# Query norm of a hybrid decoder step, moved from a stage of its own into the mixing projection

## What is computed

```python
def rms_norm(x, g):
    y = x * rsqrt(mean(x * x, axis=-1) + 1e-6)
    return y * g
...
h = x + merged @ w_mix_out                      # mixing projection, 1024 x 1024
q = rms_norm(h, norm_mem_q_g) @ w_q             # queries, 1024 x 1024
s = (q . k) * 256 ** -0.5 ; p = softmax(s)      # 4 heads of 256, 256 memory rows
h = h + (p . v) @ w_o
h = h + hier_moe(rms_norm(h, norm_ffn_g), ...)  # 32 experts, all weights are read
```

## Time and profile before

| | |
|---|---|
| time, median of 3 runs | 1238.07 us (1235.44 to 1240.53) |
| profiled execution, its own time | 1244.22 us |
| its span | 1242.5 us |
| PE busy | 1159.0 us, 93% |
| DVE busy | 497.1 us, 40% |
| ACT busy | 317.6 us, 26% |
| HBM read | 286.76 MB |

### The profile page before, as it was taken

How to read it: one execution, slowest core, us unless ns; L and a number is a source line. 1 busy time by engine, 2 the same in 40 slices (tenths; PEclk the granted TensorE clock), 3 DMA queues, 4 the chain that set the end, 5 groups by cost and what they waited for, 6 DMA issues and landing times.

```text
span 1242.5 us, 16696 instructions
## 1 busy us (share of the span) xinstructions
PE 1159.0 (93%) x6784; PEld 755.6 (61%) x6784; DVE 497.1 (40%) x876; ACT 317.6 (26%) x602; POOL 54.2 (4%) x83
## 2 busy tenths in 40 slices
PE   4999999999989899987889999999999999999995
PEld 3787568987759899987877874333333333333331
DVE  4989857018754544554445432111121121112103
ACT  3042123233225434543343331111101111011002
POOL 1504000010000000000000000000000000000000
PEclk9999999999859899989899989999999999999998
DMA  9381431033314276352245638999999999999961
GB/s 273 82 220 69 169 135 70 1 117 119 102 51 152 73 280 232 137 182 90 90 177 208 255 154 343 422 421 422 421 421 420 421 421 421 421 421 421 420 285 42
DMA packets 90695, 297.74 MB, mean 240 GB/s; under 512 B 20973, under 2 KB 30921, under 8 KB 65916
## 3 DMA queue, kind: packets, MB, share of 16 engines
q1 hardware_dynamic: 87844, 288.25, 60.5%
q0 software_dynamic: 2256, 7.80, 1.9%
q10 hardware_dynamic: 520, 0.62, 0.1%
HBM read 286.76 MB, written 9.90 MB: 239 GB/s over the span
## 4 chain that ended last, share of the span: by engine, by line
issue 70%; PE 22%; DVE 5%; ACT 1%; DMA 0%; ACTq 0%; POOL 0%; DVEq 0%; POOLq 0%
PE bank L1240 7%; PE bank L1249 2%; PE bank L1225 2%; PE bank L1397 2%; PE bank L1526 2%; PE bank L1520 1%; PE bank L1402 1%; PE bank L1374 1%; PE bank L1443 1%; PE bank L1312 1%; PE bank L1510 1%; DMA work<-in_ssd_d_dram 0%; ACTq L735 0%; DVE work L1949 0%; PE bank L1345 0%
## 5 line engine op out<-in xcount | busy, mean ns | idle before, releaser
L1780 PE MATMUL bank<-ring,work 128*64 128x512 f32 x752 | 200.4, 598 | 0.1
L1547 PE MATMUL bank<-ops,usplit 128*128 128x320 f32 x416 | 132.8, 319 | 11.9 <-DVE usplit L2248 4.9
L1240 PE MATMUL bank<-work,ring 128*128 128x320 f32 (+1 forms) x512 | 136.6, 425 | 0.5 <-DVE work L1949 0.5
L1548 PE MATMUL bank<-ops,usplit 128*128 128x320 f32 x416 | 131.9, 317 | 0.0
L1549 PE MATMUL bank<-ops,usplit 128*128 128x320 f32 x416 | 131.7, 317 | 0.0
L1240 PEld LDWEIGHTS bank<-work,ring 128*128 128x128 f32 x512 | 97.2, 192 | 34.7 <-issue 2.6
L1780 PEld LDWEIGHTS bank<-ring,work 128*64 128x64 f32 x752 | 58.2, 136 | 95.1 <-issue 93.4
L2248 DVE TENSOR_TENSOR usplit<-ring,usplit 128x2048 fp32r<-128x2048 f32 x34 | 77.9, 2291 | 85.1 <-ACT usplit L946 84.7
L1795 PE MATMUL bank<-ring,work 128*64 128x512 f32 x400 | 106.0, 597 | 0.7 <-ACT work L1157 0.7
L1780 PE MATMUL bank<-work 128*64 128x512 f32 x272 | 90.3, 597 | 0.0
L1547 PEld LDWEIGHTS bank<-ops,usplit 128*128 128x128 f32 x416 | 81.3, 195 | 12.9 <-issue 12.7
(11 more groups left out here) (457 smaller groups left out, 1567.1 us busy)
## 6 DMA issues: line engine op xcount, KB each, us to landing
ring<-in_w_exp_down_dram SPq DMA_DIRECT2D x50, 1024.0 KB, 13.9
ring<-in_w_exp_gate_dram SPq DMA_DIRECT2D x49, 1024.0 KB, 13.8
ring<-in_w_exp_up_dram SPq DMA_DIRECT2D x45, 1024.0 KB, 15.2
ring<-in_w_in_dram SPq DMA_DIRECT2D x11, 2048.0 KB, 8.2
work<-in_w_exp_up_dram SPq DMA_DIRECT2D x19, 1024.0 KB, 14.5
work<-in_w_exp_gate_dram SPq DMA_DIRECT2D x15, 1024.0 KB, 15.9
work<-in_w_exp_down_dram SPq DMA_DIRECT2D x14, 1024.0 KB, 12.3
ring<-in_w_glu_dram SPq DMA_DIRECT2D x4, 2048.0 KB, 9.1
```

Source lines behind the costliest of these rows:

```text
L1240: ins = nc.tensor.matmul(b[:, 0:N], wv[:, k, P * (m % 4):P * (m % 4 + 1)], src[:, k, 0:N], start=(k == 0), stop=(k == KT - 1))
L1547: nc.tensor.matmul(b[:, 0:T], wh, hi_[:, k], start=(k == 0), stop=False)
L1548: nc.tensor.matmul(b[:, 0:T], wh, lo_[:, k], start=False, stop=False)
L1780: ins = nc.tensor.matmul(psum[part][ES * x:ES * (x + 1), :], xs[i % 2][:, kk, x], wt[x][:, k], start=(kk == 0), stop=(kk == KT - 1))
```

## The change

The rows are no longer scaled before they are turned. As soon as a mixing unit is added to `h`, ScalarE squares its part of the rows, TensorE turns the two blocks of 128 features that the unit made (`rows_in`, jobs `fq`), ScalarE writes block times gain as the high part and VectorE the low part, both out of the bank. The queries are made of these unscaled rows. The root is taken meanwhile, put on the diagonal of three 128x128 tiles (`diag`), and spread over all partitions by a product with ones (job `rsb`); ScalarE copies that with the factor 1/16, and VectorE multiplies each finished query by it while emptying its bank. Queries 0 and 1 first do blocks 0 to 5, then, when blocks 6 and 7 have been turned, the rest. The first sample's keys are turned after the first scores, and the third sample's load waits until the last query was emptied.

```diff
@@ plan()
-    j += [f"mx{u}{c}" for u in range(4) for c in range(NC)]
-    j += [f"hq{c}{h}" for c in range(NC) for h in range(2)]
-    j += [f"q{m}" for m in range(4)] + [f"kt0{i}" for i in range(4)] + [f"q{m}" for m in range(4, KT)]
-    j.append("sc0")
+    for u in range(4):
+        j += [f"mx{u}{c}" for c in range(NC - (u == 3))]
+        if u:
+            j += [f"fq{2 * u - 2}", f"fq{2 * u - 1}"]
+    j += [f"mx3{NC - 1}", "q0", "fq6", "fq7", "q1", "rsb"] + [f"q{m}" for m in range(2, KT)]
+    j += ["sc0"] + [f"kt0{i}" for i in range(4)]
@@ SyncE
-                if BLOCKS[n][0] == "q0":
-                    sp.wait_ge(s["glu_used"], KT)
-                    load_memory(2)
+            done(sp, f"q{KT - 1}")
+            load_memory(2)
@@ ScalarE
-            for i in range(4):
+            def rows_hi(k):
+                got(act, f"fq{k}")
+                act.activation(q_hi[:, k], bank(f"fq{k}")[:, 0:T], ACT.Copy, scale=vec[:, V_Q + k:V_Q + k + 1]).then_inc(
+                    s["q_hi"], 1)
+
+            for i in range(3):
                 split_unit(unit_of("mx0") + i + 1)
-
+                for c in range(NC):
+                    unit_squares("mx", 0, i, c)
+                if i:
+                    rows_hi(2 * i - 2)
+                    rows_hi(2 * i - 1)
+            split_unit(unit_of("q0"))
             sqrt_table()
-            done(act, f"mx3{NC - 1}")
-            squares(act, 5)
+            unit_squares("mx", 0, 3, 0)
+            unit_squares("mx", 0, 3, 1)
+            rows_hi(4)
+            rows_hi(5)
+            unit_squares("mx", 0, 3, 2)
             root(2)
-            for c in range(NC):
-                for hf in range(2):
-                    done(act, f"hq{c}{hf}")
-                    v = (slice(None), slice(4 * hf, 4 * hf + 4), slice(P * c, P * c + ROWS[c]))
-                    act.activation(q_hi[v], hn2T[v], ACT.Copy).then_inc(s["q_hi"], 1)
+            rows_hi(6)
+            rows_hi(7)
+            split_unit(unit_of("q0", 1))
+            got(act, "rsb")
+            emptied(act.activation(rsb, bank("rsb")[:, 0:T], ACT.Copy, scale=1.0 / 16), "rsb")
...
-            for m in range(KT):
-                if m % 2 == 0:
-                    split_unit(unit_of("q0") + m // 2 + 1)
-                if m == 4:
-                    keys(0)
-                got(act, f"q{m}")
-                emptied(act.activation(qT[:, m], bank(f"q{m}")[:, 0:T], ACT.Copy, scale=1.0 / 16), f"q{m}")
+            for i in range(1, 4):
+                split_unit(unit_of("q0") + i + 1)
             split_unit(unit_of("o0", 1))
+            keys(0)
@@ TensorE
+            def rows_in(k):
+
+                b = take(f"fq{k}")
+                for c in range(NC):
+                    done(pe, f"mx{k // 2}{c}")
+                    ins = tr(b[:, P * c:P * c + ROWS[c]], h[0:ROWS[c], c, P * k:P * (k + 1)], ROWS[c])
+                end(ins, f"fq{k}")
+
...
+            b0 = take("q0")
+            queries(0, b0, 0, 6)
+            rows_in(6)
+            rows_in(7)
+            b1 = take("q1")
+            queries(1, b1, 0, 6)
+            end(queries(0, b0, 6, KT), "q0")
+            end(queries(1, b1, 6, KT), "q1")
+            b = take("rsb")
+            pe.wait_ge(s["diag"], 1)
+            for c in range(NC):
+                R = ROWS[c]
+                ins = nc.tensor.matmul(b[:, P * c:P * c + R], ones[0:R, :], diag[0:R, c, 0:R], start=True, stop=True)
+            end(ins, "rsb")
@@ VectorE
+            def rows_lo(k):
+                dve.wait_ge(s["q_hi"], k + 1)
+                got(dve, f"fq{k}")
+                ins = STT(out=q_lo[:, k], in0=bank(f"fq{k}")[:, 0:T], scalar=vec[:, V_Q + k:V_Q + k + 1],
+                          in1=q_hi[:, k].bitcast(F32), op0=ALU.mult, op1=ALU.subtract)
...
+            for c in range(NC):
+                ins = TS(diag[:, c], ident[:, :], rs[:, c:c + 1], None, ALU.mult)
+            ins.then_inc(s["diag"], 1)
             dve.memset(psum[6][:, :], 0.0)
             dve.memset(psum[7][:, :], 0.0).then_inc(s["zeroed"], 1)
...
+            split_unit(unit_of("q0", 1))
+            done(dve, "rsb")
+            for m in range(KT):
+                if m % 2 == 0 and m:
+                    split_unit(unit_of("q0") + m // 2 + 1)
+                got(dve, f"q{m}")
+                emptied(TT(qT[:, m], bank(f"q{m}")[:, 0:T], rsb, ALU.mult), f"q{m}")
```

More of the change, by code:

```diff
@@ L1615, in keys @@
                     end(ins, f"kt{bb}{i}")
-            for m in range(KT):
-                if m == 4:
-                    keys(0)
+            for m in range(2, KT):
                 proj_split("q", m, q_hi, q_lo)
@@ L2313, in _, with added @@
             dve.wait_ge(s["ld_h"], 32)
+            def rows_lo(k):
[3 more added lines that the diff above has]
+                          in1=q_hi[:, k].bitcast(F32), op0=ALU.mult, op1=ALU.subtract)
+                ins.then_inc(s["q_lo"], 1)
+                dve.wait_ge(s["q_lo"], k + 1)
+                dve.sem_inc(free[BANK[f"fq{k}"][0]], 1)
+            def added(i, c):
+                R, job = ROWS[c], f"mx{i}{c}"
+                got(dve, job)
+                v = h[0:R, c, 256 * i:256 * (i + 1)]
+                emptied(STT(out=v, in0=bank(job)[0:R, 0:256], scalar=0.5, in1=v, op0=ALU.mult, op1=ALU.add), job)
             for i in range(4):
```

115 lines of the change are left out of this document (48 added, 67 removed).

## The result

Changed kernel: 1232.47 us, median of 16 executions (1225.21 to 1239.62). Kernel before, in the same comparison: 1240.79 us, median of 16 (1235.44 to 1245.25). Ratio 0.9935, 95% interval 0.9913 to 0.9957: 8.3 us faster. The profiled execution of the changed kernel took 1236.91 us (span 1235.2, mean granted clock 0.959), the one of before 1244.22 (span 1242.5, clock 0.958).

A forecast was written before the change was run, and what follows sets the result against it. TensorE, busy 93%, was taken as the bound, with the expert weight stream ending the run. Saving 13.0 us in mixing and queries less 2.1 at the attention start gave 10.9, from 1238.07 to 1227.2 us; range 1222.8 to 1232.5.

The forecast's parts named there:

- Mixing and queries: From mixing end to query end: 34.5 us in place of 47.5, a saving of 13.0 us.
- a wait: Before query 2, TensorE waits 1.0 us for VectorE's weight split, which stands behind Newton steps, diagonals and bank fills.
- The spread: Three fp32 matmuls spreading the root behind queries 0 and 1: taken as 0.7 us, bounds 0.6 to 1.1.
- Rival 2: ScalarE's squares and copies delay the splits and TensorE waits at each unit: saved 7, 1231 us; chance 0.12.
- Attention start: From query end to first probabilities turned: key copies delay the sample scores, cost 2.1 us, bounds 0.4 to 3.8.
- the slow piece of the upper bound: At the attention start, a slow piece like the second sample's keys (3.58 us against 1.91) on top: cost 3.8 us.
- One for one: Ahead of the expert weight stream, each us lost or saved moves the end by as much.
- The starting level: The saving of 10.9 us was set against the median shown, 1238.07 us, giving 1227.2.
- no change: Whole kernel's time within 0.5%, 6.2 us: 1231.9 to 1244.3 us; chance 0.09.
- The third sample's load: Keys and values loaded behind the queries, keys landing in 9.0 us: hidden by 7 us.
- The first expert load: Start of the expert weight stream after attention: 11 us earlier.

The follow-up runs named there:

- e4: Changed kernel with three squares of whole rows in place of twelve small ones; 1234.92 us, ratio 0.9927 to the kernel before.
- 11.2 profiles: Profiles of the unedited changed kernel with about 11.2 us from first mixing matmul to VectorE's 64-row addition of mixing unit 0; ends 679.35 to 679.38 us behind that addition.
- e9: Changed kernel run again, no edit; 1229.63 us, ratio 0.9916 to the kernel before.
- e15: Changed kernel run again, no edit, one execution; 1226.66 us.
- e8: Changed kernel with 20 useless transposes ahead of the output projection; 1233.5 us, ratio 0.9894 to the kernel before.
- e16: Kernel before run again, no edit, one execution; 1242.46 us.
- e7: Changed kernel with 22 useless transposes in TensorE's wait ahead of the sample scores; 1231.28 us, ratio 0.9888 to the kernel before.
- e1: Changed kernel run again, no edit; 1233.04 us, ratio 0.992 to the kernel before.

## Where the prediction failed, and what in it was right

**Mixing and queries: right.** Predicted 13.0 us. Up to the first scores it is 12.3. Nothing waits inside mixing (28.96 us busy of 28.96; predicted 28.8, the 25.3 of before and 3.5 for three pairs), nothing inside the first two queries (8.03 us, predicted 8.2), no half clock at the queries' start, a wait of 1.11 (1.0). The spread took 0.97 in place of the 0.7 that I took; it lies near my upper bound (1.1), not the lower (0.6).

**Rival 2, ScalarE late: no.** In the profile after ScalarE squares, copies, and then splits the next weights from 566.20; VectorE's part runs from 568.15 to 570.4, where 570.8 was forecast, and TensorE does not wait for it. e4 shows that the number of squares changes nothing on the path.

**Attention start: mis-sized.** Predicted a cost of 2.1 us, bounds 0.4 to 3.8. Measured as the time from the first scores to the first probabilities, 5.93 in the kernel before: 9.34, thus 3.4, in the three 11.2 profiles, 2.1 in e9 (8.00), 3.2 in e15 (9.08). The chain of rows is the one predicted, and 2.1 is its length at full clock to the tenth. What came on top is the slow piece of the upper bound, which I had kept out of the likeliest value. As a mean over the five profiles of the changed kernel the cost is 3.1.

**One for one: wrong.** The step that failed is the one of the first part: the stream of expert weights "ends the run", and "what the stretch ahead of it loses or saves moves the end one for one". From the first scores to the first expert matmul the profiles before, after and of e9 have:

```profile
629.39:755.92 126.53, 114.39 (x918) 91.25 (x918) 58.15 (x171) 49.49 (x115) 0.00 (x0) 0.93 0.54 210
```

```profile
616.84:748.59 131.75, 119.69 (x934) 95.73 (x934) 59.29 (x172) 50.50 (x117) 0.00 (x0) 0.90 0.59 228
```

```profile
615.94:741.26 125.32, 113.03 (x933) 90.28 (x933) 59.25 (x172) 50.40 (x117) 0.00 (x0) 0.95 0.61 237
```

TensorE's idle time is 12.1, 12.1 and 12.3 us, so no wait was added. What differs is how long the same work keeps it busy, at a granted clock of 0.93, 0.90 and 0.95. Of the 5.2 us between before and after, 1.9 are the 16 transposes of keys that moved into this stretch (918 and 934 records), and the other 3.3 the clock. In the router alone the kernel before took 31.05 us, against 33.37 in the profile after and 29.49 in e9 (rows above):

```profile
724.87:755.92 31.05, 26.44 (x125) 19.11 (x124) 11.06 (x57) 10.42 (x22) 0.00 (x0) 0.78 0.73 295
```

e8 moved the output projection by 2.1 us and the end by nothing, and the same program crosses the router in 29.49 or 33.37 us. A saving at the norm moves everything behind it against the half clock stretches, and part of it can be given back there, or more come on top. From the first probabilities to the end the kernel before takes 607.2 us (609.4 in e16), the changed one 609.0 in three profiles, 604.9 and 604.8 in two, with the same work. None of my terms or rivals held that spread of some 4 us. And the stream does not end the run: behind the first expert matmul TensorE waits for no transfer in the trace after, and the last weights land 38 us before the end. From the first expert matmul to the end it is 486.6 us in all four profiles of before and in three of the changed kernel, though from the first expert load to the end it is 553.0 in the profile before and 555.3 in the one after. In e9 and e15, where a half clock stretch reaches past that matmul, it is 487.5, TensorE's busy time 0.9 us more and its idle time the same. So the end follows the first expert matmul, and with it whatever the clock did to TensorE on the way there. As a mean over profiles, the end moved from 686.8 (four) to 677.4 (five): 9.4 us, near the 10.9.

**The starting level: 2.7 us.** I set the sum against 1238.07, the median of three executions. It was 1240.79 over 16 in the comparison. Over the six comparisons here the kernel before has a median of 1241.57 (80 executions, 1234.69 to 1247.55) and the changed one 1231.52 (38, 1225.21 to 1239.62), 10.1 us apart, interval 7.5 to 11.7. The saving of 10.9 is within that, though just outside the first comparison's own interval (5.3 to 10.8 us by its ratio). The time of 1227.2 was 5.3 us too low against 1232.47, half of it from the level (2.7) and half from the saving of that comparison (8.3, 2.6 short). That 1232.47 still lies in the range I gave, which ended at 1232.5, is luck: the level, which was no term of the sum, and the saving missed by 2.7 and 2.6 us, and both together just fitted in. It lies also in what I had called no change (1231.9 to 1244.3, chance 0.09), though by the ratio the kernel is faster by 0.65%, more than the 0.5% of that band. I had seen that the profiled run was 6.15 above the median shown and called it of no effect. It should have told me that three executions of this kernel don't fix a median to better than 3 us.

**Others.** The third sample's load, issued at 616.82, held TensorE up nowhere: it has no wait for a transfer in attention. The first expert load was issued 9.6 us earlier in the profile's own time (679.87 against 689.50), where 11 were forecast.

**What stays open**: which of the two, the phase of the slow stretches at the start of mixing or something that goes with it, decides a course (only the association was seen, in 20 profiles), and whether filling an idle time with useless transposes pays in all courses.

## What to carry to other kernels

A norm ahead of a projection can be taken off the path by projecting the unscaled rows and multiplying the finished result: here that, with blocks handed on as they are ready, gave some 10 of the 12.3 us, the half clock that went with the gap included, and spreading it over the stage before 0.7. Before you say that a saving reaches the end one for one, look at what the clock did in the stages between. Read an edit's worth at the next common mark, where it repeated to 0.02 us in the changed kernel here, and only then at the end. Do not read a difference of less than 5 us at the end from one profile of each kernel, nor set a forecast against the median of three executions if single ones differ by 5.

## What the runs showed of the hardware that was not expected

- The same program, with all marks up to the first scores equal to 0.02 us, took 612.9 to 618.4 us from there to the end (e9, e1), with the same waits to 0.3 us up to the first expert matmul; what differs is the granted clock. Over the 38 executions of the changed kernel the time and the mean granted clock correlate at -0.95: 1225.24 us at 0.969, 1239.62 at 0.958.
- Work added to a wait did not lengthen the run: 22 transposes more in e7, and the following 16 matmuls took 1.07 us where they took 1.92 in the profiles of the changed kernel in that course; 20 more in e8, and the end stayed at 679.38.
- Three fp32 matmuls with a 128x128 operand (six records) took 0.97 us at full clock, against 0.6 for as many transposes (half of the 1.15 for six).
